# Modulation of the second and third blocks computed inside the convolution stage of the first

## What is computed

```python
def _ada(cvec, w, b):                        # first block, two matrices of 1024 x 3072
    m = jax.nn.silu(cvec) @ w + b
    return jnp.split(m, 3, axis=-1)

def second_block(x, c, ..., w_ada, b_ada, ...):   # w_ada is 1024 x 6144
    mod = (cond @ w_ada[l] + b_ada[l])[:, None, :]
    ...

def third_block(x, c, w_ada, b_ada, ...):         # w_ada is 1024 x 6144
    mod = cond @ w_ada[i] + b_ada[i]
    ...

def _conv_mixer(h, w_in, b_in, dw, dw_b, ln_g, ln_b, w_out, b_out, conv_fn):   # in the first block
    p = h @ w_in + b_in                      # 512 x 1024 @ 1024 x 6144
    a, gl, gate = jnp.split(p, 3, axis=-1)
    u = a * jax.nn.sigmoid(gl)
    u = conv_fn(u, dw, dw_b)                 # 31 taps, each channel by itself
    u = jax.nn.silu(_layernorm(u, ln_g, ln_b))
    return (u * jax.nn.silu(gate)) @ w_out + b_out
```

## Time and profile before

| | us |
|---|---|
| median of three runs | 4483.79 (4483.04 to 4493.4) |
| the profiled execution, as timed | 4492.18 |
| its span in the profile | 4490.5 |
| PE busy | 3949.0 |
| DVE busy | 1801.9 |
| ACT busy | 1263.8 |
| modulation phase, from its first DMA issue to its last write to `mod` | 28.5 to 234.9 |
| convolution phase, from its first product to its last | 1415.6 to 1928 |

### The profile page before, as it was taken

One profiled execution on the slowest core, in us unless ns is written; L12 is line 12 of the kernel. 1 busy time (PEld: TensorE's weight loads), 2 busy tenths in 40 slices (PEclk: granted clock), 3 DMA queues, 4 the chain that ended last, 5 costly groups with the idle time before them and its releaser, 6 DMA issues. The chain is left out here.

```text
span 4490.5 us, 58283 instructions
## 1 busy us (share of the span) xinstructions
PE 3949.0 (88%) x23763; PEld 2643.4 (59%) x23763; DVE 1801.9 (40%) x3005; ACT 1263.8 (28%) x2143; POOL 605.9 (13%) x326
## 2 busy tenths in 40 slices
PE   6789999999968997977889987999786777799998
PEld 2356666666655443435446555788555657687876
DVE  1023444544431999213222332443226536434431
ACT  0133343333332111223212333332223131323321
POOL 0000000000021000001000003344330020243442
PEclk7789999999979998988988998999898888999999
DMA  8911111111023221011212112333120010232331
GB/s 316 387 55 43 47 47 37 42 42 42 23 66 89 75 75 52 19 53 38 66 32 57 43 29 84 85 95 98 38 54 2 11 48 3 71 94 85 94 93 62
DMA packets 484578, 313.33 MB, mean 70 GB/s; under 512 B 28364, under 2 KB 441605, under 8 KB 484390
## 3 DMA queue, kind: packets, MB, share of 16 engines
q1 hardware_dynamic: 484390, 310.67, 23.2%
HBM read 308.54 MB, written 2.10 MB: 69 GB/s over the span
## 5 line engine op out<-in xcount | busy, mean ns | idle before, releaser
L548 PE MATMUL hg_bank<-hT,hg_w 128*128 128x512 f32 x1024 | 447.3, 592 | 0.0
L1009 PE MATMUL cv_bank<-hT,cv_w 128*128 128x512 f32 x768 | 334.1, 596 | 14.1 <-DMA cv_w<-in_conv_w_in_dram 14.1
L548 PEld LDWEIGHTS hg_bank<-hT,hg_w 128*128 128x128 f32 x1024 | 193.3, 190 | 223.6 <-issue 221.9
L1083 DVE SCALAR_TENSOR_TENSOR conv_u<-cv_pad,vec,conv_u 128x512 f32<-128x512 f32 x480 | 318.7, 742 | 0.0
L2796 POOL TENSOR_TENSOR tl_wl<-tl_w,tl_wh 128x1024 fp32r<-128x1024 f32 (+1 forms) x104 | 246.0, 2367 | 524.7 <-ACT tl_wh L2907 524.6
L1009 PEld LDWEIGHTS cv_bank<-hT,cv_w 128*128 128x128 f32 x768 | 146.8, 191 | 199.8 <-issue 184.8
L2907 ACT ACTIVATE tl_wh<-tl_w 128x1024 fp32r<-128x1024 f32 (+1 forms) x104 | 108.5, 1043 | 357.2 <-PE tl_bank L2833 354.9
L1863 POOL TENSOR_TENSOR mp_wl<-mp_w,mp_wh 128x1024 fp32r<-128x1024 f32 x72 | 173.0, 2404 | 243.9 <-ACT mp_wh L1928 243.9
L2831 PE MATMUL tl_bank<-tl_room,tl_wh 128*128 128x512 f32 x464 | 188.3, 406 | 12.6 <-POOL tl_wl L2796 11.8
L2833 PE MATMUL tl_bank<-tl_room,tl_wl 128*128 128x512 f32 x464 | 182.7, 394 | 0.0
L845 POOL TENSOR_TENSOR ho_wl<-ho_w,ho_wh 128x2048 fp32r<-128x2048 f32 x8 | 36.6, 4581 | 1072.5 <-ACT ho_wh L877 1072.5
(11 more groups left out here) (665 smaller groups left out, 7845.5 us busy)
## 6 DMA issues: line engine op xcount, KB each, us to landing
ada_w<-in_w_ada_dram SPq DMA_DIRECT2D x24, 2048.0 KB, 19.7
hg_w<-in_hgrn_w_in_dram SPq DMA_DIRECT2D x80, 512.0 KB, 3.8
mp_w<-in_w_mlp_dram SPq DMA_DIRECT2D x64, 512.0 KB, 4.0
ada_w<-in_ada_w_dram SPq DMA_DIRECT2D x12, 2048.0 KB, 19.8
cv_w<-in_conv_w_in_dram SPq DMA_DIRECT2D x48, 512.0 KB, 4.0
tl_w<-in_w_ffn_in_dram SPq DMA_DIRECT2D x44, 512.0 KB, 3.9
at_w<-in_w_in_dram SPq DMA_DIRECT2D x24, 512.0 KB, 4.0
tl_w<-in_w_in_dram SPq DMA_DIRECT2D x20, 512.0 KB, 3.9
```

The lines of the kernel that those rows point to most:

```text
L548: ins = pe.matmul(bank[:, 0:w], W[m][:, k, :], src[:, k, 0:w], start=(k == 0), stop=(k == KD - 1))
L1009: ins = pe.matmul(ps[n % RING][:, :], W[n % SLOTS][:, k * P:(k + 1) * P], K.hT[:, k, :], start=(k == 0), stop=(k == KD - 1))
L1083: ins = dve.scalar_tensor_tensor(o, x, by, o, ALU.mult, ALU.add)
```

## The change

The two matrices of the second and third blocks leave `modulation_phase`, which keeps 12 of its 36 units. The other 24 units are computed in `conv_phase` as 48 units of 256 columns (`NA`), 1 MB each, in two buffers (`AW`), with two PSUM banks of their own in turn. For that `RING` goes from 7 to 5. A unit is eight matmuls of 256 columns (M), a copy on ACT, two turning matmuls (T, after the next unit's M) and a small copy on ACT (`keep`); one DVE operation at the end of the phase adds the bias to all of them. PE takes the units between tiles: `units_of` gives tile 2 three, tile 3 two, tile 4 three and so on to tile 16, and the ten that are left to tile 17. The GATE product of tile i moves to tile i + 2 (`BEHIND`), so tiles 0 and 1 have two products each, and tiles 16 and 17 one each. DVE makes the pad of the next pair's first tile eight taps before the end of a pair instead of after it. The eight semaphores that this needs are taken beside the pool.

```diff
@@ modulation_phase
-    mats = [(inp["ada_w"][0], 6), (inp["ada_w"][1], 6), (inp["w_ada_2"][0], 12), (inp["w_ada_3"][0], 12)]
+    mats = [(inp["ada_w"][0], 6), (inp["ada_w"][1], 6)]
@@ conv_phase
-    SLOTS, RING = 12, 7
+    SLOTS, RING = 12, 5
-    LAG = 5
+    LAG, BEHIND = 5, 2
+    by_tile = [[(kind, j) for kind, j in ((SIG, i), (A, i), (GATE, i - BEHIND)) if 0 <= j < NT_ and (kind == GATE or i < NT_)]
+               for i in range(NT_ + BEHIND)]
+    AC, AW = 256, 2
+    NA = 2 * 6 * DM // AC
+    EVEN = 5
+    units_of = [[] for _ in range(NT_ + BEHIND)]
+    for a in range(NA):
+        units_of[min(BEHIND + 2 * a // EVEN, NT_ + BEHIND - 1)].append(a)
@@ SP
+                def load_ada(a):
+                    if a >= NA:
+                        return
+                    if a >= AW:
+                        sp.wait_ge(ada_sum, a - AW + 1)
+                    half, c = divmod(a * AC, 6 * DM)
+                    sp.dma_start(aw[a % AW][:, :, :], ada[half][:, :, c:c + AC]).then_inc(ada_in[a % AW], 16)
+                for n in range(SLOTS):
+                    load(n)
+                for a in range(AW):
+                    load_ada(a)
+                n = SLOTS
+                for i in range(NT_ + BEHIND):
+                    for _ in by_tile[i]:
+                        if n < 3 * NT_ + NT_:
+                            load(n)
+                            n += 1
+                    for a in units_of[i]:
+                        load_ada(a + AW)
@@ PE
+                def turn(a):
+                    pe.wait_ge(ada_copied, a + 1)
+                    for j in range(AC // P):
+                        ins = pe.matmul(ps[RING + (a + 1) % 2][:, AC + 4 * j:AC + 4 * j + 4], sums[:, a % 2, j * P:(j + 1) * P], pick[:, :],
+                                        start=True, stop=True)
+                    ins.then_inc(ada_turn, 1)
+
+                def modulation(a):
+                    pe.wait_ge(ada_in[a % AW], 16 * (a // AW + 1))
+                    if a == 0:
+                        pe.wait_ge(cond_ok, 6)
+                    if a >= 2:
+                        pe.wait_ge(ada_copied, a - 1)
+                    if a >= 3:
+                        pe.wait_ge(ada_kept, a - 2)
+                    for k in range(KD):
+                        g = 32 * (k % 4)
+                        ins = pe.matmul(ps[RING + a % 2][g:g + 32, 0:AC], cond[:, k, :], aw[a % AW][:, k, :], start=(k < 4), stop=(k >= KD - 4))
+                    ins.then_inc(ada_sum, 1)
+                    if a >= 1:
+                        turn(a - 1)
...
+                    for a in units_of[i]:
+                        modulation(a)
                     if i >= LAG:
                         total(i - LAG)
-                for i in range(NT_ - LAG, NT_):
+                pe.wait_ge(ada_kept, NA - 1)
+                turn(NA - 1)
+                for i in range(NT_ + BEHIND - LAG, NT_):
                     total(i)
@@ ACT, behind the tile's sigmoid and silu
+                    for a in units_of[i]:
+                        act.wait_ge(ada_sum, a + 1)
+                        if a >= 1:
+                            act.wait_ge(ada_turn, a)
+                        act.activation(sums[:, a % 2, :], ps[RING + a % 2][:, 0:AC], ACT.Copy).then_inc(ada_copied, 1)
+                        if a >= 1:
+                            keep(a - 1)
+                keep(NA - 1)
@@ DVE
+                padded(0)
                 for j in range(NT_ // 2):
+                    padded(2 * j + 1)
                     for t in range(CW):
+                        if t == CW - 8 and 2 * j + 2 < NT_:
+                            padded(2 * j + 2)
...
+                dve.wait_ge(ada_kept, NA)
+                dve.tensor_tensor(K.mod[:, 48:48 + 2 * NA, :], turned[:, :, :].rearrange("p a (j v) -> p (a j) v", v=4),
+                                  K.vec[:, bias2:bias2 + 2 * NA].unsqueeze(2).broadcast_to((P, 2 * NA, 4)), ALU.add).then_inc(out_d, 1)
```

More of the change, by code:

```diff
@@ L963, in conv_phase @@
         bg = K.sb(st, "cv_bg", [P, KD])
+        aw = [K.sb(st, f"cv_ada{s}", [P, KD, AC]) for s in range(AW)]
+        cond = K.sb(st, "cv_cond", [P, KD, 32])
+        pick = K.sb(st, "cv_pick", [P, 4])
+        sums = K.sb(st, "cv_sums", [P, 2, AC])
+        turned = K.sb(st, "cv_turned", [P, NA, 8])
         ps = K.psum_banks(st, "cv")
@@ L979, in wait_bank @@
             else:
-                pe.wait_ge(act_free, 2 * i + (1 if kind == SIG else 2))
+                pe.wait_ge(act_free, on_act[(kind, i)] + 1)
         with nc.Block() as block:
@@ L985, in _, with load @@
                 clear_old(sp, old)
-                for n in range(3 * NT_ + NT_):
+                def load_ada(a):
[5 more added lines that the diff above has]
+                    sp.dma_start(aw[a % AW][:, :, :], ada[half][:, :, c:c + AC]).then_inc(ada_in[a % AW], 16)
+                def load(n):
                     s = n % SLOTS
@@ L995, in _ @@
                         sp.dma_start(W[s][:, :], wo[:, n - 3 * NT_, :]).then_inc(w_in[s], 16)
+                for n in range(SLOTS):
[10 more added lines that the diff above has]
+                        load_ada(a + AW)
+                for n in range(n, 3 * NT_ + NT_):
+                    load(n)
             @block.tensor
@@ L1001, in total @@
                     pe.matmul(SUM[:, :], K.ones[:, :], u[:, i, :], start=(i == 0), stop=(i == NT_ - 1)).then_inc(sum_ok, 1)
-                for i in range(NT_):
-                    for kind in (SIG, A, GATE):
-                        n = 3 * i + kind
+                def turn(a):
[18 more added lines that the diff above has]
+                        turn(a - 1)
+                for i in range(NT_ + BEHIND):
+                    for kind, j in by_tile[i]:
+                        n = at_of[(kind, j)]
                         pe.wait_ge(w_in[n % SLOTS], 16 * (n // SLOTS + 1))
@@ L1033, in _, with keep @@
             def _(act):
[L1034 to L1040, removed]
-                    act.activation(gate[:, i, :], ps[(3 * i + 2) % RING][:, :], ACT.Silu,
-                                   bias=K.vec[:, a_b + 32 + i:a_b + 33 + i]).then_inc(act_free, 1)
+                def keep(a):
+                    act.wait_ge(ada_turn, a + 1)
+                    act.activation(turned[:, a, :], ps[RING + (a + 1) % 2][:, AC:AC + 8], ACT.Copy).then_inc(ada_kept, 1)
+                for i in range(NT_ + BEHIND):
+                    for kind, j in by_tile[i]:
+                        n = at_of[(kind, j)]
+                        if kind != A:
+                            act.wait_ge(prod, n + 1)
+                        if kind == SIG:
+                            if j >= 4:
+                                act.wait_ge(pad_ok, j - 3)
+                            act.activation(sig[:, j % 4, :], ps[n % RING][:, :], ACT.Sigmoid,
+                                           bias=K.vec[:, a_b + 16 + j:a_b + 17 + j]).then_inc(act_free, 1)
+                        elif kind == GATE:
+                            act.activation(gate[:, j, :], ps[n % RING][:, :], ACT.Silu,
+                                           bias=K.vec[:, a_b + 32 + j:a_b + 33 + j]).then_inc(act_free, 1)
+                    for a in units_of[i]:
[6 more added lines that the diff above has]
+                keep(NA - 1)
                 act.wait_ge(bg_ok, 1)
```

34 lines of the change are left out of this document (26 added, 8 removed).

## The result

The changed kernel takes 4500.01 us (median of six runs, 4497.36 to 4504.02); the kernel before took 4486.78 in the same comparison (six runs, 4480.45 to 4494.96). The ratio is 1.003, with an interval of 1.0018 to 1.0041: **slower by 0.3%**. The forecast was 4461, with a range to 4496. Both the sign and the range were wrong. Ratios compare fast executions; one of ten with the fill ahead of the wait (8165.45 us) and one of ten of the phase reorganised without units (6219.56) are left out of them.

A forecast was written before the change was run, and what follows sets the result against it. The prediction took transfers to bound the modulation phase and PE, nearly tied with DVE, the convolution phase. It summed -130.2 + 78.4 + 28.3 + 0.8 = -22.7 us, 4483.8 to 4461, with an 8-in-10 range of 4425 to 4496.

The forecast's parts named there:

- The gain: Modulation phase, bound by its transfers, loses 24 loads of 5.43 us each: -130.2 us.
- The price of a unit (u): Convolution phase: each moved unit costs PE 1.65 us (1.49 to 2.1), plus 0.2 for each tile with units.
- Rival 2: Units cost 2.0 us through changes of form and a load takes 6.2: 4487 us, no clear change; chance 0.18.
- The stall of a three-unit tile (s): PE waits 3.2 us before the third unit, its load landing 5.3 us after issue; 5.0 with its clock.
- SP's queue clean: SP's product loads wait only for same-tile products done by then, with buffers twelve deep; no cost was added.
- The clock behind a stall: After each PE stall in the convolution phase, the lower granted clock costs 1.8 us, ends 0 and 3.4.
- Up to the last pad: First convolution product to product A of tile 15, whose pad starts the last pair: 334.2 becomes 412.6 us, +78.4.
- From the last pad to the mean: End of the convolution phase: 44.6 becomes 72.9 us, +28.3, with ten units in a row taking 31.
- The sum: Whole kernel: -130.2 + 78.4 + 28.3 + 0.8 = -22.7 us, from 4483.8 to 4461.
- rival 3: Every tile's block of units, not only those with a stall, is followed by 1.2 GHz: 4499 us, slower; chance 0.14.
- Rival 1: Cheap stalls: loads land in 4.4 to 4.9 us and the clock hardly falls: 4432 us; chance 0.20.
- rival 4: DVE stays the convolution phase's bound, so the whole -130 shows: 4347 to 4354 us; chance 0.03.

The follow-up runs named there:

- the fill ahead of the wait: Changed kernel plus six dense 512-column matmuls on PE before the wait for the third unit's load: 4474.97 us against 4482.69 for the kernel before, ratio 0.998.
- the other order: Changed kernel with each tile's last 512 KB weight load issued behind its modulation loads: 4480.09 us against 4486.93 for the kernel before, ratio 0.9989.
- the dense fill: Changed kernel plus six dense 512-column matmuls after the wait, before the third unit: 4539.41 us against 4488.38 for the kernel before, ratio 1.0114.

## Why the prediction was wrong

The structure of the forecast was right, and two terms in it had the wrong size.

- **The gain**: forecast 130.2, measured 133.4. Right.
- **The price of a unit (u)**: forecast 1.65 and 0.2 a tile, 57.1 up to the last pad. One M starts 1.54 us after the other (M 1.07, T 0.61, with the records overlapping), an entry costs 0.1, and with loads in time the 33 units take 372.2 - 320.5 = 51.7: 5.4 us in favour. The Trainium skill (TensorEngine Tiling (Array Packing), section Tiling Modes, key properties) says that a change of mode drains TensorE; no gap of that kind is to be seen at the changes of form, two in a unit: where loads are in time, PE's records leave no us free (320 of 320, 380 of 380), and a drain too short to show between them is inside the 1.54 and 0.1. Rival 2's units at 2.0 fell; its late load was the right direction, and 6.2 was still too early.
- **The stall of a three-unit tile (s), the first failed step.** "Estimate 5.3 from issue to landing": the awaited loads took 7.7 on the mean in the changed kernel (8.2 is the median of all 48), so that seven waits took 40.6 us where the forecast had 22.4, +18.2, and the eighth 6.04 instead of 3.2. The estimate itself is right for a load with nothing just ahead of it: 5.4 with the other order. What it left out is the load ahead. The working of the forecast went from PE's side, from the sum to the issue, and called SP's queue clean because no wait in it blocks. It never asked which other bytes are under way at the moment of the issue, and the third weight load goes out right then. The Trainium skill (DMA: Bandwidth & Descriptors, section Anatomy of one DMA) has 2.0 us plus bytes over 436 GB/s; the estimate from it is 4.4 us for this load. The page gives that fit for transfers that GpSimd issues, which the prediction did not say, and these are issued by SyncE. No median here agrees: 5.4 with nothing just ahead, 8.2 over the loads of the changed kernel.
- **The clock behind a stall, the second failed step.** Forecast 1.8 us each, with an upper end of 3.4, from rows 8. In the changed kernel's rows it is 3.7, and against the run with three buffers 3.6, +12.8 over seven tiles; taking it away alone gave 3.2 a tile at least. Rows 8 showed 6.7 and 4.2 us of mostly 1.2 GHz behind a stall, and here 7.5 us of slow work lie behind the wait of 6.32, and 8.5 behind one of 3.08. I chose the middle between none and the trace's worse row, though both rows of the trace spoke for a price.
- **Up to the last pad** then: 18.2 + 12.8 - 5.4 = 25.6, and the rows have 438.15 - 412.6 = 25.5. The runs give nearly the same by another way: 324.1 for the phase without units, 33 x 1.46 = 48.2 for the units, 40.6 of waits and 25.6 of clock from the changed kernel's rows are 438.5.
- **From the last pad to the mean**: 81.5 against 72.9. The wait in tile 16 with its clock is about 9.5 instead of 5.0: +4.5. The ten units take 35.1 us instead of 31 (+4.1). Their pairs stand 7.25 to 7.43 us apart (forecast 7.0), and the last pair takes 5.6 instead of 3, as the row stays at 1.2 GHz.
- **The sum.** -22.7, +25.5, +8.6 and -3.2 for the larger gain are +8.2; the spans differ by +9.3 and the medians by 13.2. About 1 us is left in what follows the mean, which I did not trace to a cause. The 3.9 between spans and medians are the executions that were profiled: 5.4 above the median of its six for the kernel before, 1.4 for the changed one.

The pattern foretold is there: waits in even tiles alone, M near 1.0 and T near 0.6, DVE waiting for PE, no clock below 1.00 behind odd tiles. That refutes rival 3, which had a time of 4499 for a reason that isn't the one at work: a right number from a wrong mechanism, by luck. Rival 1 had the loads too early and the clock too light: behind waits of 3.1 us, shorter than both stalls of rows 8, the clock fell all the same; rival 4 would have had DVE without idle time.

What stayed open: why a 512 KB load issued about 1 us ahead delays the awaited 1 MB load by 2.3 us (the eight waits fell from 46.6 to 28.6 in all), a little more than the 1.8 us that the forecast gave its own transfer. And whether the narrow matmuls alone keep the clock down; the row of three buffers speaks for it, the dense fill only in part.

## What to carry to other kernels

Before moving loads into a phase whose DMA share is low, ask for each what else is issued in the microseconds around it on the same queue, and how much work lies between the freeing of its buffer and its use; a free DMA share says nothing of a single load's landing. Spread moved work so that each load has a long piece of work to land under: one unit behind each product, or one buffer more, turned +0.3% into -1.5%, and up to the last pad the rests (but for one of 0.3 us) and the lower clock behind them went at once. Where a bound engine is made to rest, count the clock at the worst rows of the trace, not at a mean with zero.

## What the runs showed of the hardware

- A 1 MB load (1 KB pieces) landed in 5.1 to 5.4 us with nothing issued just ahead of it, in 6.5 to 8.3 with a 512 KB load issued about 1 us earlier on the same queue, and in 8.6 to 9.6 when another 1 MB load had also gone out 0.8 to 1.5 us before it. With three buffers in turn the median was 9.2, and PE waited for it only once.
- The granted clock fell to 1.2 GHz within rests of 3.08 and of 6.32 us and stayed there for 10.2 us both times, so that a rest half as long had the same slow stretch, with more work in it. Such a stretch cost 3.6 us in the changed kernel.
- Behind a rest, seven units of narrow matmuls back to back stayed at 1.2 GHz for 20.5 us with PE busy for 19.95, while the same matmuls between products ran for 380 us at 2.4 GHz. That PE was busy did not bring the clock back there. With six dense matmuls behind a rest of 4.5 to 6.7 us, five of eight slow stretches were 6.8 us and three 10.2. Why is open.
